# Sparse attention inside a macaron block: rounded score passes, values for four heads at once, and the compressed branch moved to the front

## What is computed

```python
def reference(x, ...):
    x = x + 0.5 * swiglu(rmsnorm(x, ffn1_norm[i]), ffn1_wg[i], ffn1_wu[i], ffn1_wd[i])
    x = x + hybrid_mixer(rmsnorm(x, mix_norm[i]), w_in[i], ...)
    x = x + 0.5 * swiglu(rmsnorm(x, ffn2_norm[i]), ffn2_wg[i], ffn2_wu[i], ffn2_wd[i])
    return rmsnorm(x, final_norm)

def hybrid_mixer(h, ...):
    (c_h, c_b, c_c, q, k_c, v_c, k_s, v_s, k_w, v_w, g) = jnp.split(h @ w_in, cuts, axis=-1)
    y_conv = short_conv_mixer(c_h, c_b, c_c, conv_w)
    kc, vc = compress(rope(k_c), ...), compress(v_c, ...)
    y_attn = nsa_attention(q, kc, vc, k_s, v_s, k_w, v_w, sigmoid(g))
    y = jnp.concatenate([rmsnorm(y_conv), rmsnorm(y_attn)], axis=-1)
    return y @ w_out
# in nsa_attention, per head: three softmaxes p of q.k, and
#   o = g0 * (p_cmp @ v_c) + g1 * (p_slc @ v_s) + g2 * (p_win @ v_w)
```

## Time and profile before

| what | before |
|---|---|
| median of 3 runs | 1903.28 us (1902.91 to 1903.29) |
| the profiled execution | 1902.96 us, of which the span of the trace is 1901.2 us |
| TensorE matmuls busy | 1886.6 us, 99% of the span |
| VectorE busy | 1021.4 us, 54% |
| ScalarE busy | 853.9 us, 45% |
| GpSimd busy | 202.5 us, 11% |
| granted TensorE clock | 0.999 of full speed |
| bytes moved by DMA | 362.53 MB, 191 GB/s over the span |

### The profile page before, as it was taken

One profiled execution on the slowest core, in us unless ns is written; L12 is line 12 of the kernel. 1 busy time (PEld: TensorE's weight loads), 2 busy tenths in 40 slices (PEclk: granted clock), 3 DMA queues, 4 the chain that ended last, 5 costly groups with the idle time before them and its releaser, 6 DMA issues.

```text
span 1901.2 us, 23218 instructions
## 1 busy us (share of the span) xinstructions
PE 1886.6 (99%) x8538; PEld 1544.2 (81%) x8539; DVE 1021.4 (54%) x1092; ACT 853.9 (45%) x1067; POOL 202.5 (11%) x376
## 2 busy tenths in 40 slices
PE   9999999999999999999999999999999999999998
PEld 7888888888888888887778778888888888888886
DVE  5555555545554444555665775555555555544544
ACT  6444444444444444444454645444444444444443
POOL 1111222111100000000000000111111112200000
PEclk9999999999999999999999999999999999999999
DMA  7666676666655555554335545666666666676654
GB/s 259 206 204 193 203 217 212 207 199 191 220 180 196 198 189 185 177 177 123 115 96 167 188 155 177 211 207 191 203 211 207 206 199 198 208 232 192 198 190 142
DMA packets 197212, 362.53 MB, mean 191 GB/s; under 512 B 18772, under 2 KB 23616, under 8 KB 197024
## 3 DMA queue, kind: packets, MB, share of 16 engines
q1 hardware_dynamic: 183264, 349.22, 58.3%
q0 software_dynamic: 11648, 12.02, 2.2%
q10 hardware_dynamic: 2240, 0.47, 0.1%
HBM read 348.01 MB, written 2.10 MB: 184 GB/s over the span
## 4 chain that ended last, share of the span: by engine, by line
PE 97%; DVE 2%; ACT 1%; issue 0%; ACTq 0%; DVEq 0%
PE ps L486 31%; PE ps L488 31%; PE ps L487 31%; PE ps L507 2%; PE ps L644 1%; PE ps L664 1%; DVE w_lo L1184 1%; PE ps L645 0%; ACT w_hi L860 0%; PE ps L536 0%; PE ps L737 0%; DVE p_h L1459 0%; ACT junk L887 0%; DVE x L1255 0%; ACT hT_hi L874 0%
## 5 line engine op out<-in xcount | busy, mean ns | idle before, releaser
L1184 DVE TENSOR_TENSOR w_lo<-raw,w_hi 128x1024 fp32r<-128x1024 f32 x656 | 793.1, 1222 | 715.8 <-ACT w_hi L860 714.7
L860 ACT ACTIVATE w_hi<-raw 128x1024 fp32r<-128x1024 f32 x656 | 688.3, 1060 | 734.0 <-PE ps L488 727.7
L486 PE MATMUL ps<-w_hi,hT_hi 128*128 128x512 f32 x1760 | 689.1, 392 | 1.2 <-DVE w_lo L1184 1.1
L488 PE MATMUL ps<-w_hi,hT_lo 128*128 128x512 f32 x1760 | 685.2, 389 | 0.0
L487 PE MATMUL ps<-w_lo,hT_hi 128*128 128x512 f32 x1760 | 685.1, 389 | 0.0
L486 PEld LDWEIGHTS ps<-w_hi,hT_hi 128*128 128x128 f32 x1760 | 330.7, 188 | 69.9 <-issue 1.4
L488 PEld LDWEIGHTS ps<-w_hi,hT_lo 128*128 128x128 f32 x1760 | 330.3, 188 | 69.3
L487 PEld LDWEIGHTS ps<-w_lo,hT_hi 128*128 128x128 f32 x1760 | 330.5, 188 | 67.1
L448 POOL DMA_DIRECT2D gu_raw<-gu_sq x352 | 187.0, 540 | 872.8 <-DVE gu_sq L1246 796.5
L486 PE MATMUL ps<-w_hi,guT_hi 128*128 128x512 f32 x704 | 274.3, 390 | 0.0
L488 PE MATMUL ps<-w_hi,guT_lo 128*128 128x512 f32 x704 | 274.0, 389 | 0.0
(11 more groups left out here) (195 smaller groups left out, 783.7 us busy)
## 6 DMA issues: line engine op xcount, KB each, us to landing
raw<-in_ffn_wg_dram SPq DMA_DIRECT2D x176, 512.0 KB, 4.4
raw<-in_ffn_wu_dram SPq DMA_DIRECT2D x176, 512.0 KB, 4.7
raw<-in_ffn_wd_dram SPq DMA_DIRECT2D x176, 512.0 KB, 4.4
raw<-in_w_in_dram SPq DMA_DIRECT2D x88, 512.0 KB, 3.6
raw<-in_w_out_dram SPq DMA_DIRECT2D x32, 512.0 KB, 4.5
gu_raw<-gu_sq POOLq DMA_DIRECT2D x352, 32.0 KB, 4.3
raw<-in_cmp_k_w_dram SPq DMA_DIRECT2D x8, 256.0 KB, 3.3
raw<-in_cmp_v_w_dram SPq DMA_DIRECT2D x8, 256.0 KB, 4.0
```

The costliest lines, as they stand in the source:

```text
L486: mm(o, x_hi, w_hi[:, s, kk, :], start=first and kk == 0, stop=False)
L488: ins = mm(o, x_lo, w_hi[:, s, kk, :], start=False, stop=last and kk == GK - 1)
L860: act.activation(w_hi[:, c % SLOTS, :, :], raw[:, c % SLOTS, :, :], ACT.Copy).then_inc(hi_ready, 1)
L1184: tt(w_lo[:, s, :, :], raw[:, s, :, :], w_hi[:, s, :, :].bitcast(F32), ALU.subtract).then_inc(lo_ready, 1)
```

## The change

1. **Order of groups.** The compression inputs (`KC`) are projected first and the compression weights are streamed between the groups of `KW`. Compression, its scores, softmax and values are done before the first tick. `TICK0` moves from `CC_UP,1` to `CH_UP,2`.
2. **Scores.** Query halves are stored as `q_st`: 64 rows of rounded query and 64 rows of the rest. Keys are stored twice over the rows, rounded (`k_hi`) and rest (`k_lo`). A score is two float32r passes over 128 rows.
3. **Values.** After four heads VectorE scales their probabilities (`weigh`), TensorE transposes four heads at a time (one fill of bank 4 per key tile), ScalarE rounds each fill (`prob_high`), VectorE takes the rest (`prob_low`), and TensorE multiplies the values [hi | rest] as the stationary operand by 512 columns, twice per key tile. The result is already transposed; ScalarE moves the halves onto the same rows (`shift_halves`) and VectorE adds them to the compressed branch in `yT` (`attended`).
4. **Banks.** All convolution transposes of the ticks share bank 5 with the attention output.
5. **Norm of the attention.** Its squares are summed by GpSimd and a product with ones; the 16 transposes of the output (`att_transposes`) go.
6. **Room.** `x` is written to DRAM before the queries need its place and read back after the last scores (16 transfers of 256 KB on SyncE's queue).

```diff
-IN_COL = [3072, 3584, 4608, 5120, 4096, 2560, 512, 1536, 0, 1024, 2048]
-Q0, Q1, KS, KW, KC, CC_UP, CH_UP, CB_UP, CH_LO, CB_LO, CC_LO = range(N_IN)
+IN_COL = [4096, 3072, 3584, 4608, 5120, 2560, 512, 1536, 2048, 0, 1024]
+KC, Q0, Q1, KS, KW, CC_UP, CH_UP, CB_UP, CC_LO, CH_LO, CB_LO = range(N_IN)
...
+    order = [(("in", jb), j) for jb in range(KW) for j in range(JD)]
+    for j in range(JD):
+        order += [(("in", KW), j), (("cmp",), j)]
+    order += [(("in", jb), j) for jb in range(KW + 1, N_IN) for j in range(JD)]
...
-TICK0 = AT[("in", CC_UP), 1]
+TICK0 = AT[("in", CH_UP), 2]
+PARK_AT = [AT[("in", Q0), 2] + 3 * n for n in range(2 * NDC)]
+BACK_AT = [OUT0 - 3 + n for n in range(2 * NDC)]
...
...
+def fill_at(m):
+    u, n = divmod(m - 5, GRP)
+    if u < 0 or u >= UNITS:
+        return None
+    if key_tiles(u) == GRP:
+        return u, n
+    return (u, n // 2) if n % 2 == 0 else None
...
+def output_at(m):
+    u, n = divmod(m - 9, GRP)
+    return u if n == 0 and 0 <= u < UNITS else None
...
+    extra = {11: ("cu", 2), 12: ("cu", 3), 19: ("cb", 2), 20: ("cb", 3), 32: ("cu", 0), 34: ("cu", 1)}
...
-            uses.append((extra[m], 6 + (m + 1) % 2))
+            uses.append((extra[m], 5))
...
-                mm(o, qT[rows_, jp * GRP + r, t * P:t * P + P], kT[rows_, jp, :, 0:nk], start=True, stop=False)
-                mm(o[:, :, nk - P:nk], ident_b[:, :], causal_b[:, :, :], start=False, stop=True).then_inc(full[bank], 1)
+                mm(o, q, k_hi[:, j, :, 0:nk], start=True, stop=False)
+                mm(o[:, :, nk - P:nk], ident_b[:, :], causal_b[:, :, :], start=False, stop=False)
+                mm(o, q, k_lo[:, j, :, 0:nk], start=False, stop=True).then_inc(full[bank], 1)
...
+                for f in range(last + 1):
+                    br, kt = divmod(f, t + 1)
+                    v = v_st[:, kt, br, j, :, :].rearrange("p s d -> p (s d)")
+                    mm(ps[:, bank, :], v, pT_hi[:, f, :], start=f == 0, stop=False)
+                    ins = mm(ps[:, bank, :], v, pT_lo[:, f, :], start=False, stop=f == last)
...
+            def k_high(jp):
...
+                for par in range(2):
+                    src = ps[par * HD:par * HD + HD, bank, :].rearrange("p (b t) -> p b t", b=2)
+                    for dst in (par, 1 - par):
+                        ins = act.activation(k_hi[dst * HD:dst * HD + HD, 2 * jp + par, :, :], src, ACT.Copy)
...
+            def prob_low(u, f):
...
+                dve.wait_ge(pT_hi_ready, use - USE["PT", 0, 0][1] + 1)
+                tt(pT_lo[:, f, :], ps[:, bank, :], pT_hi[:, f, :].bitcast(F32), ALU.subtract).then_inc(free[bank], 1)
+            def weigh(u):
...
+                seq(tt(coef[:, :, :], den[:, t, GRP * j:GRP * j + GRP, 1:3], sums[:, m:m + GRP, :], ALU.mult))
+                seq(nc.vector.reciprocal(coef[:, :, :], coef[:, :, :]))
+                p = prob[:, u % 2, :, 0:2 * nk].rearrange("p r (b n) -> p r b n", b=2)
+                tt(p, p, coef[:, :, :].unsqueeze(3).to_broadcast([P, GRP, 2, nk]), ALU.mult).then_inc(p_scaled, 1)
```

More of the change, by code:

```diff
@@ L645, in scores @@
[L645 to L668 removed]
+                q = q_st[:, jp * GRP + r, par, t * P:t * P + P]
@@ L704, in conv_square_sum, with att_square_sum @@
                 ins.then_inc(full[bank], 1)
+            def att_square_sum():
+                bank, u = USE["ass",]
+                pe.wait_ge(att_sq_sum, 1)
+                to_bank(bank, u)
+                for t in range(NT):
+                    for c in range(2):
+                        ins = mm(ps[:, bank, t:t + 1], att_sq[:, c, t * P:t * P + P], ones, start=c == 0, stop=c == 1)
+                ins.then_inc(full[bank], 1)
             def hid_transposes():
@@ L709, in hid_transposes @@
                 to_bank(bank, u)
-                transposes(bank, [(n * P, scr[:, n * P:n * P + P]) for n in range(2)])
+                transposes(bank, [(n * P, hid[:, 0, n * P:n * P + P]) for n in range(2)])
             def compressed_kv():
@@ new lines, in mixer @@
+                put(started(CH_UP) + 5, lambda: compressed_operand(0), lambda: compressed_operand(1))
+                put(started(CH_UP) + 7, lambda: compressed_values(0), lambda: compressed_values(1))
+                put(started(CH_UP) + 8, lambda: compressed_values(2), lambda: compressed_values(3))
+                for m in range(TICKS):
+                    if fill_at(m) is not None:
+                        put(TICK0 + 2 + m, lambda m=m: prob_high(*fill_at(m)))
+                    if m < NT * HEADS:
+                        put(TICK0 + 2 + m, lambda m=m: exps(m))
+                    if output_at(m) is not None:
+                        put(TICK0 + 2 + m, lambda u=output_at(m): shift_halves(u))
@@ L1116, in mixer @@
+                for n in (2, 3):
+                    put(TICK0 + 1 + NT * HEADS + n, lambda n=n: conv_operand(n))
                 o = OUT0
[L1117 to L1123 removed]
@@ L1129, in mixer @@
+                put(o + 7, lambda: root(RS_CONV), lambda: att_square(1))
+                for n in range(4):
+                    put(o + 8 + n, lambda n=n: att_operand(n))
+                put(o + 14, lambda: root(RS_ATT))
                 for n in range(NDC - 1):
@@ new lines, in attended @@
+            def attended(u):
+                t, j = divmod(u, KV)
+                bank, use = USE["O", u]
+                dve.wait_ge(half_shifted, u + 1)
+                if u == 0:
+                    for n in range(KV):
+                        dve.wait_ge(free[USE["Oc", n][0]], USE["Oc", n][1] + 1)
+                y = yT[:, 2 * j:2 * j + 2, t * P:t * P + P]
+                seq(tt(shifted[:, :, :], shifted[:, :, :], y, ALU.add))
+                o = ps[:, bank, :].rearrange("p (q two m) -> p two q m", two=2, m=P)
+                tt(y[0:HD, :, :], o[0:HD, 0, :, :], shifted[0:HD, :, :], ALU.add)
+                tt(y[HD:P, :, :], o[HD:P, 1, :, :], shifted[HD:P, :, :], ALU.add).then_inc(free[bank], 1)
+                if u == UNITS - 1:
+                    dve.wait_ge(free[bank], use + 1)
+                    dve.sem_inc(y_att_ready, 1)
```

586 lines of the change are left out of this document (342 added, 244 removed).

## The result

The change made the kernel slower, by less than one per cent: 1917.89 us, median of four runs (1916.63 to 1919.04), against 1903.28 us before. The ratio is 1.0077, 95% interval 1.0059 to 1.0094. That is 14.6 us; the forecast was 4.7 us, 1908, with a range from 1889 to 1924. Figures read from a trace are of one execution of each kernel (1918.74 us for the changed one, span 1916.5), which can lie a few us off the median.

The account below looks back on a forecast made before the run. A VectorE-ScalarE program-order loop was to take over the bound from TensorE in both halves of the ticks: waits 31.6 us less 27.6 saved, +4.0 on 1902.96, 1907.0, stated as 1908 us; range 1889 to 1924.

Parts of the forecast that it names:

- the forecast case: Whole kernel: the VectorE-ScalarE loop binds in both halves of the ticks; 1908 us, chance 0.55.
- What bounds the kernel: Attention ticks: TensorE bound before; afterwards a program-order loop between VectorE and ScalarE (`w_hi`, `w_lo`, minimum, exponential) binds, 4.9 us a tick.
- The loop's sum: Exponential 0 to 31: VectorE-ScalarE steps added start to start, 66.7 us for short rows and 85.0 for long, 151.7 together.
- The signs: In the trace: TensorE about 97% busy, waits 25 to 35 us; wrong if bank 5 waits lack `w_lo` or score passes exceed 0.23.
- TensorE's saving: Scores, values and output transposes: 23.6 us less TensorE work, from 9.6, 4.3, 8.7 and 1.0 us.
- the 4.0 of my sum: Whole kernel: TensorE waits of 31.6 us less 27.6 saved, so 4.0 us slower than the kernel before.
- The waits that compression was to take with it: Output groups: with compression moved out, 4.0 of TensorE's 4.6 us of waits counted as gone.
- Bank 5: Rival, ticks 9, 12, 13, 17, 20, 21: waits for bank 5 add 12 to 18 us; 1923 us, chance 0.16.
- The loop binding in one half only: Rival, ticks: only long rows wait, half of the waits, 16 us; 1891 us, chance 0.14.
- The clock: Rival, ticks: short pauses bring TensorE to 1.2 GHz for a quarter of the work, 40 us more; 1948, chance 0.03.
- TensorE keeping the bound: Rival, ticks: room between slots hides the VectorE-ScalarE loop; 1878 us, chance 0.12.
- Parking at nothing: Writing `x` to DRAM and reading it back, 16 transfers spread over weight groups: costs nothing.

Follow-up runs that it names:

- cutting the loop: On the changed kernel, each tick's exponentials stand one weight group later in ScalarE's order; 1885.12 us.
- shortening it: On the changed kernel, `score_min` stands ahead of `prob_low` and `weigh` in VectorE's order in every tick; 1898.95 us.
- lengthening its ticks by 11.4: On the changed kernel, each `prob_low` is preceded by the same product written to a scratch tile, 24 in all; 1932.14 us.
- the kernel with the loop cut and all bursts spread: Changed kernel with exponentials one group later, plus second halves of `k_high` and `k_low`, hidden transposes, compressed steps and gate weights one group later; 1878.57 us.
- the last experiment: On the kernel of 1878.57 us, second `k_low`, `v_low` behind it and the second output-stage `ycT_lo` product pair one group later; 1881.75 us.
- the one with the waits filled: On the changed kernel, 76 products of a tile of zeros put on TensorE ahead of its eight longest waits; 1915.87 us.

## Why the prediction was right, and what in it was not

The measured 1917.9 us lies inside the range of 1889 to 1924, but outside the 1901 to 1915 that I gave for the forecast case alone.

*What bounds the kernel.* Right, and shown from four sides: cutting the loop gave 32.8 us, shortening it 18.9, lengthening its ticks by 11.4 cost 11.0, and a TensorE at full clock gained 1.5 in them.

*The loop's sum.* 151.7 us were forecast for 31 ticks, 154.8 measured; by halves 66.7 against 68.2 and 85.0 against 86.5. The steps were read one by one from the kernel before, and they held: 4.46 us is an ordinary long-row tick, 7.11 one with the product (2.29 against 2.25). The ticks that I named as signs, 4.8 and 5.3 us, came out as 4.55 and 5.41; the first did not even agree with my own sum (66.7 / 15 = 4.45).

*The signs.* Waits of 25 to 35 us were named, nearly all in the ticks; those of the table of waits are 32.2, of which 22.2 stand in the 31 ticks, and the wait at the keys was 3.5 us instead of 2.9. TensorE's busy share fell to 98%, not 97. Two signs of being wrong appeared. The waits on bank 5 were not one, since moving them away changed nothing. Score passes dearer than 0.23 us came too (next paragraph).

*TensorE's saving.* A little larger than 23.6 us. Long-row scores are 0.67 us, as forecast, but by luck: each pass is 0.32 and the mask between them 0.03, not 0.23 and 0.21, and the two errors cancel. Short-row scores are 0.44, not 0.57: 2.1 us more saved. With the loop cut, a short-row tick takes 3.7 us and a long-row tick 4.0, where I had 3.8 and 4.3 for TensorE alone. Full cover was put at 1875.7 us before any wait; the kernel with 5.9 us of waits for `w_lo` left ran in 1878.57. The rule that I quoted from the Trainium skill (Perfetto Trace Analysis, Identifying the Most-Contended Engine), work on the engine with the highest occupancy, came within 3 us of the kernel with the loop cut and all bursts spread (within 10 of the one with the loop cut alone) and missed the changed kernel by 42 us. It is a rule about amounts, and this was an order.

*Where the other 10 us come from.* My terms, against the profiled executions, whose spans lie 15.3 us apart (1916.5 and 1901.2), 11.3 more than the 4.0 of my sum:

- Ahead of the key transposes' end, 3.7 us more than forecast: 1.7 of it is the clock behind the wait for `hid`, 0.9 that wait itself (2.0 against 1.1), 1.1 the three waits for `w_lo` at 789, 796 and 864 us (1.9 against 0.8).
- From there to the end of exponential 0, 18.3 us against 17.2: `k_low` took 0.70 a piece where I had 0.60.
- The 31 ticks, 3.1 more.
- Behind exponential 31, 22.0 us against 20.6.
- The waits that compression was to take with it, 1.7 less than forecast. Of the five waits of the kernel before, 4.6 us, only three stood in the output groups, 3.5 us, and one of 1.1 us came new there, at 1105 us. So 2.3 us went, not 4.0. (Its waits were also not all of 4.6: 0.5 us for `prob` and 1.2 at the start of the program stand beside them.)

That is 11.0 of the 11.3 us. No single step failed: five terms were each a little short, all in the same direction. I took small values for the copies, as the 0.60 for `k_low`, counted too many waits as gone, and left the clock out of the sum.

*The rivals.* Bank 5 had 0.16 and would have been the wrong reason for nearly the right number: 1923 was its price. It is refuted by moving it. The loop binding in one half only, at 0.14, is refuted by the two halves of the ticks, 68.2 and 86.5 us, both longer than my sums for the loop and both far above the 55.8 and 64.3 of the kernel with the loop cut. The clock had 0.03 at 40 us. It did fall, so it was more likely than I said, but the price was wrong too: 11.3 us of work lost, of which 2 to 4 us count. TensorE keeping the bound at 1878 us was refuted for the change, and is what the order with all bursts spread reaches. Parking at nothing was right as far as it was tested.

## What to carry to other kernels

When one engine is 99% busy and two others half, write down for each loop across engines who waits for whom in program order, and add its steps start to start; if the sum per round is near the busy engine's time per round, work taken from the busy engine buys nothing until that order is changed. A wait's name says who came last, not what it costs: move the suspect, and see whether the time moves or only the name. And an order of queues has to be chosen anew after each change: the one-line edit that is worth 33 us here costs 11 in the kernel before.

## What the runs showed of the hardware

The low level of TensorE's clock costs only where TensorE is on the path: with it gone from the ticks, 7.9 us of work, they got 1.5 us shorter. In the changed kernel it fell five times, behind pauses of 2.0, 3.5, 3.0, 3.1 and 3.0 us, to a pass pitch of 0.43 instead of 0.23 us, for some 3 to 7 us each (an estimate from the means above). Behind two others, of 2.4 and 2.3 us at 961 and 1003 us, it stayed full. The Trainium skill (TensorE: Matmul & The Clock Gate, A second HAM failure mode) tells of a clock that swings when TensorE idles briefly and often. In one stretch that is not borne out: between 1040 and 1062 us the changed kernel paused in every tick, for 0.5 us mostly and once for 1.8, up to the long pause at the end, and the row is at 1.00:

```profile
1040.00:1062.00 22.00, 18.08 (x84) 13.27 (x84) 13.82 (x20) 10.70 (x26) 0.00 (x0) 1.00 0.25 72
```

Nor does the length of a pause decide. The wait of 2.0 us for `hid` was followed by the low level in the changed kernel, and by the full one in the kernel with the exponentials later. In the kernel before with its exponentials later, pauses of 1.66 and 1.43 us were followed by the low level (884 and 966 us) and two of the same lengths by the full one (924 and 1013 us). And it fell without any pause, busy 10.00 of 10 us, behind the 32 products of 32 columns of the compressed branch: in the last experiment and in the one with the waits filled, while the same products left it at 1.00 in the changed kernel. What decides it, no run here shows.
